# Two pairs of stages made into one each: gate, turn and project the scan outputs; bring back, norm and project the routed rows

## The reference, cut to what matters

```
# end of layer 0's state-space mixer, for all 768 tokens (y: 768 x 2048)
y = y * silu(z)
x = x + gate * (rmsnorm(y, norm_w) @ out_w)            # out_w: 2048 x 1024
x = x + gate2 * experts(...)                           # each expert's rows are added to its tokens' rows

# start of layer 1's attention, for all 768 tokens
h = rmsnorm(x, norm1_w) * (1 + scale) + shift
q, k, v = split(h @ qkv_w)                             # k and v: 512 columns, q: 1024 columns (latents only)
k = rmsnorm per head, rotated; q likewise; then attention
```

## Time and profile before

| | |
|---|---|
| median of 3 runs | 3486.58 us (3485.42 to 3488.64) |
| the profiled execution | 3485.87 us |
| its span, first to last instruction | 3484.1 us, 1.8 us less than its time |
| mean granted TensorE clock | 0.954 of full speed |
| TensorE, matmuls | 3106.6 us busy, 89% |
| VectorE / ScalarE / GpSimd | 1358.7 / 983.1 / 829.1 us busy |

### The profile page before, as it was taken

One profiled execution on the slowest core, in us unless ns is written; L12 is line 12 of the kernel. 1 busy time (PEld: TensorE's weight loads), 2 busy tenths in 40 slices (PEclk: granted clock), 3 DMA queues, 4 the chain that ended last, 5 costly groups with the idle time before them and its releaser, 6 DMA issues. The chain is left out here.

```text
span 3484.1 us, 40894 instructions
## 1 busy us (share of the span) xinstructions
PE 3106.6 (89%) x16241; PEld 1965.0 (56%) x16241; DVE 1358.7 (39%) x2148; ACT 983.1 (28%) x2218; POOL 829.1 (24%) x581
## 2 busy tenths in 40 slices
PE   5999997878959999978999699898798999889998
PEld 2778885656723333326667333333676646668877
DVE  1128876774331111114764311111636853433321
ACT  3112225654131221213353211110443331432211
POOL 3333324660001101013101000000432203334443
PEclk8999998998979999998999799999999999999999
DMA  5444554433099999972403799999222224132141
GB/s 214 160 156 138 171 190 139 152 110 126 2 381 396 401 397 395 404 272 100 146 1 127 279 413 411 413 411 390 86 88 94 83 100 149 49 126 87 63 144 40
DMA packets 272042, 697.17 MB, mean 200 GB/s; under 512 B 16016, under 2 KB 62956, under 8 KB 269548
## 3 DMA queue, kind: packets, MB, share of 16 engines
q1 hardware_dynamic: 263072, 672.32, 50.9%
q0 software_dynamic: 6656, 16.78, 2.0%
q10 hardware_dynamic: 2124, 5.46, 0.4%
HBM read 647.30 MB, written 47.22 MB: 199 GB/s over the span
## 5 line engine op out<-in xcount | busy, mean ns | idle before, releaser
L728 PE MATMUL ps<-h_parts,weights_high 128*128 128x512 f32 (+3 forms) x2560 | 742.7, 375 | 28.0 <-PEq L261 13.8
L134 POOL TENSOR_TENSOR weights_low<-ring,weights_high 128x1024 fp32r<-128x1024 f32 (+1 forms) x205 | 499.0, 2437 | 708.0 <-ACT weights_high L127 697.6
L728 PEld LDWEIGHTS ps<-h_parts,weights_high 128*128 128x128 f32 (+2 forms) x2560 | 464.7, 189 | 133.2 <-issue 20.8
L728 PE MATMUL ps<-h_parts,weights_low 128*128 128x512 f32 (+2 forms) x1280 | 478.0, 373 | 0.0
L2342 PE MATMUL ps<-area 128*32 128x512 f32 (+1 forms) x1632 | 286.8, 598 | 2.6 <-ACT area L2430 2.5
L728 PEld LDWEIGHTS ps<-h_parts,weights_low 128*128 128x128 f32 (+1 forms) x1280 | 241.5, 189 | 46.5 <-issue 0.6
L127 ACT ACTIVATE weights_high<-ring 128x1024 fp32r<-128x1024 f32 (+1 forms) x135 | 140.8, 1052 | 264.0 <-PE ps L728 245.8
L2540 PE MATMUL ps<-area 128*64 128x512 f32 x832 | 191.1, 612 | 21.2 <-DMA ring<-in_moe_w 8.4
L728 PE MATMUL ps<-weights_high,h_parts 128*128 128x512 f32 x608 | 195.8, 400 | 7.1 <-PEq L261 7.1
L2342 PEld LDWEIGHTS ps<-area 128*32 128x32 f32 (+1 forms) x1632 | 84.2, 124 | 189.8 <-issue 187.0
L1192 DVE SCALAR_TENSOR_TENSOR area<-area,param_columns 128x772 f32<-128x772 f32 x128 | 182.3, 1424 | 10.3 <-issue 0.9
(11 more groups left out here) (496 smaller groups left out, 4754.9 us busy)
## 6 DMA issues: line engine op xcount, KB each, us to landing
area<-in_moe_w SPq DMA_DIRECT2D x103, 2048.0 KB, 24.5
ring<-in_moe_w SPq DMA_DIRECT2D x54, 2048.0 KB, 24.8
weight_parts<-in_moe_w SPq DMA_DIRECT2D x35, 2048.0 KB, 24.2
ring<-in_ada_w SPq DMA_DIRECT2D x24, 2048.0 KB, 8.7
ring<-in_ssd_in_w SPq DMA_DIRECT2D x12, 2048.0 KB, 7.9
ring<-in_w_in SPq DMA_DIRECT2D x11, 2048.0 KB, 7.9
ring<-in_w_ffn_in SPq DMA_DIRECT2D x10, 2048.0 KB, 7.7
area<-x_dram SPq DMA_DIRECT2D x12, 1024.0 KB, 4.9
```

The source lines that it names most:

```text
L134: pool.tensor_tensor(lo, views[k][:, ks, cols], hi, ALU.subtract).then_inc(self.low_p, 1)
L728: mm = pe.matmul(out, a, b, start=start and n == 0, stop=stop and n == 2)
```

## The change

The two stages at each place become one.

**First place, `gate_out`.** ScalarE and VectorE make the first four blocks of the output weights before the first tile is gated. TensorE turns tile p+1 bank by bank and between the banks multiplies tile p with those four blocks (slices 0 to 7 of 16), 24 matmuls a tile. The transposes use only banks 6 and 7 in turn, each free again when the low parts before it are made. The other 12 block steps then run as before. SP loads z first; X, the row gates and the fourth chunk of weights wait behind the last square and the last transpose.

```diff
+            for b in range(4):
+                turn(0, b)
+            for p, i in enumerate(order):
+                for b in range(4):
+                    turn(p + 1, b)
+                    pe.wait_ge(low, 4 * p + b // 2 + 1)
+                    if p == 0:
+                        pe.wait_ge(ring.low_p, b0 + b + 1)
+                    mm = product(b, i)
+                    if p == NT - 1:
+                        mm.then_inc(ring.done, 1)
+            pe.wait_ge(low, 4 * NT)
+            for m in range(CUTS, 2 * pairs):
...
         @block.scalar
+            for m in range(CUTS):
+                cut(m)
+            for p, i in enumerate(order):
+                act.wait_ge(gated, p + 1)
...
+                for b in range(4):
+                    act.wait_ge(turned, 4 * p + b + 1)
+                    act.activation(quad(parts[i][0], b), bank(b), ACT.Copy).then_inc(high, 1)
+            act.wait_ge(eps_in, 1)
+            act.activation(rstd, rstd, ACT.Sqrt).then_inc(rooted, 1)
+            for m in range(CUTS, 2 * pairs):
+                cut(m)
...
         @block.vector
+            for m in range(3):
+                cut_low(m)
+            for p, i in enumerate(order):
+                dve.wait_ge(zt_in[p % 2], 16 * (p // 2 + 1))
+                dve.tensor_tensor(y[:, i, :], y[:, i, :], zb[:, p % 2, :], ALU.mult).then_inc(gated, 1)
+                if p == 0:
+                    cut_low(3)
+                else:
+                    lows(p - 1)
```

```diff
 experts_columns, @block.sync
-            sp.wait_ge(added, a0 + a1 * E)
-            for i in range(nt):
-                sp.dma_start(X[:, i, :], env.sum_dram[layer][i * P:(i + 1) * P, :]).then_inc(back, 16)
-            sp.wait_ge(back, 16 * nt)
 project_qkv, @block.tensor
+            turn_row(0, 0)
+            turn_row(0, 1)
+            for t in range(NT):
+                for b in range(4):
+                    if b % 2 == 0:
+                        turn_row(t + 1, b // 2)
+                    pe.wait_ge(parted, 2 * t + b // 2 + 1)
...
+                    for k in (2 * b, 2 * b + 1):
+                        mm = products(pe, ps[:, t, :], tuple(x[:, k, t * P:(t + 1) * P] for x in h),
+                                      (hi[:, k % 2, :], lo[:, k % 2, :]), k == 0, k == KD - 1)
...
+            mod.products(pe, 0, at_mod[0])
 @block.scalar
+            n_ = ring.cut_after(act, cuts, views, 0, m0)
+            square(0)
+            square(1)
+            row_root(0)
+            for i in range(NT):
+                if i + 2 < NT:
+                    square(i + 2)
+                if i + 1 < NT:
+                    row_root(i + 1)
+                features_out(i)
+                if i >= 2:
+                    leave(i - 2)
 @block.vector
+                dve.tensor_scalar(xn[:, i % 2, :], X[:, i, :], ms[:, i:i + 1], None, ALU.mult).then_inc(scaled, 1)
+                if i >= 1:
+                    split(i - 1)
 build
-        gate_turn(env, top, t.y, rstd, yT)
-        ssd_out(env, top, X, rstd, yT, [md[0, 0, 2 * D:3 * D], md[0, 1, 2 * D:3 * D]], xin)
+        gate_out(env, top, t.y, rstd, yT, X, [md[0, 0, 2 * D:3 * D], md[0, 1, 2 * D:3 * D]], xin)
...
-        norm_turn(env, at + 2 * KD * TOK, X, hp, [(0, NL, mc(1, 0), mc(0, 0)), (NL, NC, mc(1, 1), mc(0, 1))],
-                  ahead=[(slice(k, k + 2), slice(0, HALF)) for k in range(0, 4, 2)])
...
-        project_qkv(env, at + 2 * KD * TOK, q, kv, hp, qT, kT)
+        project_qkv(env, at + 2 * KD * TOK, X, mc, q, kv, hp, qT, kT)
```

More of the change, by code:

```diff
@@ L1875, in _, with gate_out @@
             lows(range(4, KD))
-def gate_turn(env, base, y, rstd, parts):
+def gate_out(env, base, y, rstd, parts, X, gates, load):
     ps, ring = env.ps, env.ring_
     order = list(reversed(range(NT)))
+    kd, pairs = 2 * KD, KD
+    per = pairs - 1 + NT
     with Stage(env, base) as st:
         zb = st.sb("z_tiles", [P, 2, DI])
+        rows, o = carve(env, base, [P, 2, D]), carve(env, base + 2 * D, [P, 2, HALF])
         zt_in = [st.sem("even_z_in"), st.sem("odd_z_in")]
@@ L1902, in _ @@
[L1902 to L1924, removed]
-                act.drain()
-                act.activation(zb[:, p % 2, :], y[:, i, :], ACT.Square, scale=float(DI) ** -0.5,
-                               accum_out=rstd[:, i:i + 1]).then_inc(squared, 1)
-                for b in range(4):
-                    act.wait_ge(turned, 4 * p + b + 1)
-                    act.activation(quad(parts[i][0], b), bank(p, b), ACT.Copy).then_inc(high, 1)
-            act.wait_ge(eps_in, 1)
-            act.activation(rstd, rstd, ACT.Sqrt).then_inc(rooted, 1)
@@ L1934, in _ @@
-        @block.tensor
-        def _(pe):
-            for p, i in enumerate(order):
-                pe.wait_ge(gated, p + 1)
-                for b in range(4):
-                    if p >= 2:
-                        pe.wait_ge(low, 4 * (p - 2) + b + 1)
-                    for k in range(4):
-                        a = (4 * b + k) * P
-                        tr = pe.transpose(bank(p, b)[:, k * P:(k + 1) * P], y[:, i, a:a + P], env.ident[:])
-                    tr.then_inc(turned, 1)
-def ssd_out(env, base, X, rstd, parts, gates, load):
-    ps, ring = env.ps, env.ring_
-    kd, pairs = 2 * KD, KD
-    per = pairs - 1 + NT
-    with Stage(env, base) as st:
-        rows = st.sb("row_gates", [P, 2, D])
-        o = st.sb("product", [P, 2, HALF])
@@ L3327, in _ @@
         def _(pool):
-            for m in range(ahead, len(cuts)):
-                if m == ahead:
+            for m in range(len(cuts)):
+                if m == CUTS:
                     mod.prepare(pool)
```

165 lines of the change are left out of this document (136 added, 29 removed).

## The result

The kernel after takes 3458.61 us (median of 4 runs, 3457.72 to 3462.13) against 3486.0 us of the kernel before timed beside it: a ratio of 0.9919, 95% interval 0.9908 to 0.9931. Its profiled execution took 3457.72 us with a span of 3456.0, 28.1 us less than the span before. The forecast was 3452 in a range of 3444 to 3466, a gain of 34.2 us; measured were 27.4 (medians) or 28.1 (spans).

A forecast was written before the change was run, and what follows sets the result against it. TensorE, busy 89% of the span, was taken as the bound, with its idle time and low clock to be gained. -13.7 and -20.5 sum to -34.2 us against 3485.87: 3451.7, predicted as 3452 us, range 3444 to 3466.

The forecast's parts named there:

- The first place: Gating, turning and out projection merged into one loop, last product at 940.4 instead of 954.1 us: -13.7 us.
- the 19 turns: Groups of four transposes between products in the gating and out-projection loop: 0.52 us each, 9.9 us together.
- The second place: Rows normed, turned and projected to keys and values tile by tile, ending at 1609.9 instead of 1630.4 us: -20.5 us.
- I add 0.5: Start of the keys-and-values loop: allowance in us for GpSimd's last low block putting off VectorE's scaling.
- The bound of 2 x 1.7: Start of the keys-and-values loop: upper limit in us kept for GpSimd's low block putting off VectorE's scaling.
- The rule of the Trainium skill: VectorE and GpSimd lock a shared port; scalings wait up to 2.6 us, keys-and-values loop gains 18 instead of 20.5.
- The rest of the stage moves as a whole.: Behind the keys-and-values loop: the stage's remaining code shifts earlier together, the late chunk and root costing nothing.
- about 2 us later than now: Third weights chunk and keys' norm root, counted from the end of keys and values; covered by VectorE's 5.61 us waiting.
- A: Rival: one of the two loops is paced by engines other than TensorE; 3459 to 3469 us, chance 0.13.
- B: Rival: TensorE stays at the low clock in both loops; +43 us, 3529 us, chance 0.04.
- C: Rival: gain swallowed behind the loops by a late fifth block or keys' norm; both give 3472 us, chance 0.06.
- D: Rival: no overlap, as the first product waits for a transfer or queue; only stage ends go, 3480 us, chance 0.03.

The follow-up runs named there:

- lows on VectorE: The kernel after, with the low parts of the first four key-and-value weight blocks made by VectorE instead of GpSimd: 3448.98 us (ratio 0.9879).

## Why the prediction was right, and where it was off

**The first place** was forecast at -13.7 and gave -16.1. The first product came at 793.34 (forecast 794.3). From there to 837.6 are 44.3 us; less 33.5 of products and 1.85 lost at the low clock, the 19 turns took 8.9, or 0.47 each for the forecast 0.52: the product may follow 0.35 us after four transposes begin. The 432 products took the forecast 100.4. What was hidden stayed hidden: root and table load were over at 832.4, the fifth block's parts ready in time, no wait of TensorE before it.

**The second place** was forecast at -20.5 and gave -18.5 (35.6 less the 17.1 of everything before it). The loop was 38.6 us for 40.5: nine half turns and the clock cost 5.1 together, for 4.7 + 2.3. The start was 3.9 us late. Two steps were too small there. One is "I add 0.5" for GpSimd's port: the scaling took 4.01 us for the 1.05 + 0.5 of the sum, and without GpSimd beside it the first product came 3.4 earlier. The bound of 2 x 1.7 was kept in the range and is about what came. The other is the end of the experts' stage. The scattering ended where it was forecast (1536.13 us; 1553.2 less 17.1), but the new stage began only 3.9 us later:

```profile
1534.69 1.44 POOL L2342 DMA_INDIRECT summed_rows<-area,picked_context_half_rows  x1 [0.30 <-issue]
1540.05 2.86 SPq L3339 DMA_DIRECT2D area<-summed_rows  x6
1544.05 1.06 ACT L3457 ACTIVATE area<-area 128x1024 f32<-128x1024 f32 x1
```

The forecast had the rows' loads at 1538.9 and the first square at 1542.5 (1556.0 and 1559.6 less 17.1), and GpSimd's first subtraction, which came at 1541.21, at about 1538. So the square was 1.5 us late, and the subtractions were 3 us late and thereby lay beside the scaling instead of ahead of it. The rule of the Trainium skill, "SBUF — State Buffer" (SBUF: two separate sides), gave 18 for this place, and 18.5 came. In kind the trace agrees with it: a scaling that met a subtraction of 2.3 us took 3.3 us longer, through that one and the memset of 0.94 us behind it, so more than one instruction of GpSimd. That the total came so near is in part luck, for the rule's estimate had the stage's late start in it as little as the forecast had.

**Behind the loops** the text said "The rest of the stage moves as a whole." It doesn't. VectorE's slack before the last head norm fell from 5.61 to 1.27 us. The step that was too small is "about 2 us later than now" for the late chunk of weights and the root of the keys' norm behind it. ScalarE waits for that chunk, before (first line) and after:

```profile
1642.86 1.06 ACT L127 ACTIVATE weights_high<-ring 128x1024 fp32r<-128x1024 f32 x1 [9.87 <-DMA ring<-in_attn_qkv_w]
```
```profile
1611.83 1.06 ACT L127 ACTIVATE weights_high<-ring 128x1024 fp32r<-128x1024 f32 x1 [14.41 <-DMA ring<-in_attn_qkv_w]
```

Counted from the end of keys and values (1630.39 and 1594.83) that is 12.5 and 17.0 us, 4.5 later and not 2; from the keys' root to the first queries' norm VectorE then took 17.4 us in both. The slack was just enough. But 0.43 us on issue, where there was none before, made a wait of 1.80 into 2.16 us, and the clock fell. What failed besides is the assumption that unchanged code behind a change keeps its length. Here it differs by -1.6 to +9.3 us from attention to the end over the thirteen profiles of the table, and by 3.5 between the two of one kernel.

**The rivals.** A (loops paced by others) is out, TensorE was never idle in them. B (low clock in the loops) is out, 1.00 after 3.7 and about 2 us. The case that the Trainium skill describes in "TensorE: Matmul & The Clock Gate" (HAM oscillation — how this bites in real kernels), a short group that starts cold again because of the wait before it, is seen outside them, at L3375, L569 and L3710. C named a loss behind the loops at fifth block or keys' norm; there was one of 7.5 us, but at other places: the keys' norm was late and cost only slack. D is out.

The size of the give-back hangs on the one profile of before that it is measured against: beside the later runs the kernel before was at 3488.2 to 3491.6 us, 2 to 6 us above that profiled execution, and the kernel after at 3458.3 again. With the medians of that chip, 3489.79 and 3458.26, the gain is 31.5 us and little of the forecast 34.2 is missing.

## What to carry to other kernels

Merging "turn all, then multiply all" into one loop pays its full length when TensorE is the slowest engine per tile; count the hand-overs' engines, take the turn at what the next product waits, and look last for who shares a port with the first operation of the chain. A forecast of a stage's start should count from when every engine is through the stage ahead, not from its last instruction in the timeline. A saving of a few us in one place can't be judged from the whole kernel's time alone when clock or weight transfers shift behind it: compare the stages, and take a second profile of the same kernel as the measure. Filling a wait of TensorE with idle transposes paid 1.6 us where low-clock groups stood behind the wait (2.16 us), if the filling ends before the wait does. Where a kernel had no fall at that place (lows on VectorE, wait 1.79 us) the same filling moved the median by 1.2 us, less than can be told apart.

## What the hardware showed that was not expected

- VectorE's scaling of 1024 columns took 4.01 us instead of 0.75: it began with GpSimd's last subtraction (9.27 / 4 = 2.3 us) and ended 0.87 us after the memset behind that, so the wait was longer than either.
- A stand of 0.43 us on issue at one instruction of VectorE comes and goes with instructions added 100 us earlier in its stream, at no cost there. With it the wait before attention, the clock behind it and 1.8 us of the second place come and go; the medians were 4.5 us apart, of which the trace shows no more than this.
- The same wait (2.14 and 2.13 us) was followed by the clock at 1.2 GHz in one kernel and at 2.4 GHz in another, 5.37 against 3.67 us for eight matmuls.
- An added delay of some 2 us made the kernel 5 us faster, one of some 3 us didn't.
- Twelve transposes (2.82 us) did not bring the clock up for the eight behind them (1.91), but the next twelve took 1.68 and the products behind ran at the full rate.
